# Four accumulating banks in the first feed-forward block of a phase, two in the first projection slab

## The reference

```python
def swiglu(x, wi, wo):
    g, u = jnp.split(x @ wi, 2, axis=-1)
    return (jax.nn.silu(g) * u) @ wo

def ffn_half(h, m, k, g_norm, wi, wo):
    hn = modulate(rmsnorm_2(h, g_norm), m[3 * k], m[3 * k + 1])
    return h + 0.5 * m[3 * k + 2][:, None, :] * swiglu(hn, wi, wo)
...
        h = ffn_half(h, ml, 0, norm_g[l, 0], ffn_wi[l, 0], ffn_wo[l, 0])
        hc = ffn_half(hc, mc, 0, norm_g[l, 0], ffn_wi[l, 0], ffn_wo[l, 0])
        hn = modulate(rmsnorm_2(h, norm_g[l, 1]), ml[3], ml[4])
        hcn = modulate(rmsnorm_2(hc, norm_g[l, 1]), mc[3], mc[4])
        qa, ka, va, qb, kb, vb, uc, gl = project_tokens(hn, w_in[l], qk_g[l], cos, sin)
...
        h = h + ml[5][:, None, :] * merge_branches(ya, yb, yc, gl, w_branch[l], w_out[l])
        h = ffn_half(h, ml, 2, norm_g[l, 2], ffn_wi[l, 1], ffn_wo[l, 1])
```

## Time and profile before

| | us |
|---|---|
| median of 3 runs (lowest, highest) | 3204.87 (3204.76, 3206.72) |
| profiled execution | 3209.25 |
| its span | 3207.5 |
| TensorE matmul busy | 2942.4 (92%) |
| TensorE weight loads busy | 2384.5 (74%) |
| VectorE busy | 1560.7 (49%) |
| ScalarE busy | 1030.6 (32%) |
| GpSimd busy | 273.1 (9%) |

### The profile page before, as it was taken

The page is one execution under the profiler, slowest core; times in us unless marked ns, Lnnn a source line. Parts: engine busy times, 40 slices in busy tenths (PEclk is TensorE's granted clock), DMA queues, the critical chain, the costliest instruction groups (busy, mean ns, idle before and its releaser), DMA issues.

```text
span 3207.5 us, 54730 instructions
## 1 busy us (share of the span) xinstructions
PE 2942.4 (92%) x23653; PEld 2384.5 (74%) x23653; DVE 1560.7 (49%) x2194; ACT 1030.6 (32%) x1502; POOL 273.1 (9%) x201
## 2 busy tenths in 40 slices
PE   6998877899999989899899989999899997989899
PEld 6776565677767679777568868888688886669899
DVE  6524244232223366663764434444544457486566
ACT  3211113222222254532642332222422224264443
POOL 5123000000000000122100000000000012210000
PEclk9988888899999989999999999999999998999899
DMA  6346767999889845411012222222222221104452
GB/s 242 132 149 261 319 249 312 417 372 372 348 349 383 357 174 184 145 66 40 1 40 105 105 92 100 98 92 92 79 92 92 98 99 66 53 14 191 178 189 87
DMA packets 77067, 547.78 MB, mean 171 GB/s; under 512 B 8385, under 2 KB 10433, under 8 KB 11057
## 3 DMA queue, kind: packets, MB, share of 16 engines
q1 hardware_dynamic: 76000, 540.05, 43.4%
q0 software_dynamic: 848, 4.52, 0.4%
HBM read 637.86 MB, written 1.05 MB: 199 GB/s over the span
## 4 chain that ended last, share of the span: by engine, by line
PE 80%; DVE 11%; ACT 4%; DMA 4%; issue 1%; POOL 1%; DVEq 0%; SPq 0%; POOLq 0%; ACTq 0%
PE bank L743 58%; PE bank L1087 8%; DMA ring<-slabs 3%; PE bank L1409 2%; DVE clow L2471 1%; ACT whi L1853 1%; ACT ht L1657 1%; PE bank L792 1%; DVE tiny L2624 1%; PE bank L922 1%; PE bank L909 1%; PE bank L1497 1%; PE bank L759 1%; DVE wk L2601 1%; PE bank L1478 1%
## 5 line engine op out<-in xcount | busy, mean ns | idle before, releaser
L743 PE MATMUL bank<-hhi,whi 128*128 128x256 f32 (+1 forms) x1408 | 482.1, 342 | 31.0 <-DVE hlo L2105 30.9
L743 PE MATMUL bank<-hlo,whi 128*128 128x256 f32 (+1 forms) x1408 | 476.8, 339 | 0.0
L743 PE MATMUL bank<-hhi,wlo 128*128 128x256 f32 (+1 forms) x1408 | 472.9, 336 | 0.0
L2085 DVE TENSOR_TENSOR wlo<-ring,whi 128x2048 fp32r<-128x2048 f32 x132 | 298.7, 2288 | 223.9 <-ACT whi L1612 197.0
L743 PE MATMUL bank<-fhl,whi 128*128 128x256 f32 (+1 forms) x1408 | 351.6, 341 | 0.0
L743 PEld LDWEIGHTS bank<-hhi,whi 128*128 128x128 f32 x1408 | 267.0, 190 | 70.7 <-issue 29.6
L1612 ACT ACTIVATE whi<-ring 128x2048 fp32r<-128x2048 f32 x132 | 251.3, 1908 | 211.5 <-PE bank L743 211.3
L743 PEld LDWEIGHTS bank<-hhi,wlo 128*128 128x128 f32 x1408 | 268.3, 191 | 30.1
L743 PEld LDWEIGHTS bank<-hlo,whi 128*128 128x128 f32 x1408 | 268.4, 191 | 26.2
L1087 PE MATMUL bank<-ring,wk 128*32 128x256 f32 x4064 | 253.5, 392 | 22.9 <-DMA ring<-slabs 14.3
L743 PEld LDWEIGHTS bank<-fhl,whi 128*128 128x128 f32 x1408 | 241.0, 189 | 35.3 <-issue 5.3
(11 more groups left out here) (479 smaller groups left out, 5349.9 us busy)
## 6 DMA issues: line engine op xcount, KB each, us to landing
ring<-slabs SPq DMA_DIRECT2D x542, 1024.0 KB
wk<-slabs SPq DMA_DIRECT2D x45, 1024.0 KB, 11.5
ac<-slabs SPq DMA_DIRECT2D x16, 1024.0 KB, 11.3
wk<-mixp POOLq DMA_DIRECT2D x1, 1040.0 KB, 12.5
xt<-xT SPq DMA_DIRECT2D x1, 1024.0 KB, 6.7
xt<-ctxT POOLq DMA_DIRECT2D x1, 1024.0 KB, 6.1
out<-xt SPq DMA_DIRECT2D x4, 256.0 KB, 2.4
cst<-maskc POOLq DMA_DIRECT2D x1, 960.0 KB, 14.6
```

The costliest lines, as they stand in the source:

```text
L743: last = pe.matmul(o, a, b, start=k == 0, stop=k == len(pairs) - 1)
L2085: tt_(wlo_of(n), slab(n), whi_of(rel).bitcast(F32), ALU.subtract).then_inc(sem("wlo"), 1)
```

## The change

**Feed-forward, TensorE.** Block 0 of every phase becomes `first_block`: it waits for the low parts of both slabs, then goes over the channel tiles outermost, and for each does 8 matmuls with `hhi` (four banks, high and low weight) once `hh` is there, and 4 with `hlo` once `hl` is there. All four banks close with the last four matmuls. The counts of both slabs are paid with the first matmul of block 1.

**Projection, TensorE.** Tiles 0 and 1 are made together in the same way (`project_first`): 4 matmuls with `xhi` and 2 with `hlo` for each channel tile. The sum of squares of tile 0, which stood behind tile 1's matmuls, now stands behind the `lam` matmul.

**Low parts, VectorE.** The low part of slab 1, made after the norm before, is now made ahead of it with that of slab 0. For norm 3 both stand ahead of the reciprocal; for the phases after the output projections they stand after the drains of j = 4 and 5; for the third phase they stand in the last down slab of the second, ahead of drains 0 and 4.

```diff
                         group(bank[bank0 + ft][:, 0:T], pairs3, signal,
-                              ("hl", ph["h0"]) if b == bank0 == ft == 0 and i is None else None)
+                        group(bank[bank0 + ft][:, 0:T], pairs3, signal)
                     used(1)
+
+                def first_block():
+
+                    pe.wait_ge(sem("wlo"), w0 + 2)
+                    for k in range(KT):
+                        parts = [(bank[2 * rel + ft][:, 0:T], *halves(rel, k, ft * P, KT))
+                                 for rel in range(2) for ft in range(FT)]
+                        pe.wait_ge(sem("hh"), ph["h0"] + k + 1)
+                        for o, hi, lo in parts:
+                            mm = pe.matmul(o, hi, HHI[:, k, 0:T], start=k == 0, stop=False)
...
+                            pe.matmul(o, lo, HHI[:, k, 0:T], start=False, stop=False)
+                        pe.wait_ge(sem("hl"), ph["h0"] + k + 1)
+                        for n, (o, hi, lo) in enumerate(parts):
+                            mm = pe.matmul(o, hi, HLO[:, k, 0:T], start=False, stop=k == KT - 1)
+                            if k == KT - 1:
+                                mm.then_inc(sem("gg" if n < FT else "uu"), 1)
+                    used(2)
...
                 def step(b, i):
+                    if b == 0:
+                        first_block()
+                        return
...
+                def project_first():
+
+                    pe.wait_ge(sem("al"), count("al", N_ATT * l + 1))
+                    parts = [(bank[QB[half]][:, 0:tq], *thirds(0, half, tq)) for half in range(2)]
+                    for k in range(KT):
+                        pe.wait_ge(sem("hh"), x0 + k + 1)
+                        for o, hh, lh, hl in parts:
+                            mm = pe.matmul(o, *hh[k], start=k == 0, stop=False)
...
+                            pe.matmul(o, *lh[k], start=False, stop=False)
+                        pe.wait_ge(sem("hl"), x0 + k + 1)
+                        for o, hh, lh, hl in parts:
+                            mm = pe.matmul(o, *hl[k], start=False, stop=k == KT - 1)
+                            if k == KT - 1:
+                                mm.then_inc(sem("qp"), 1)
+                    pe.wait_ge(sem("lam"), l + 1)
+                    pe.matmul(bank[6][:, 0:2], BO64, LAMV[:, 0:2], start=True, stop=True).then_inc(sem("lamd"), 1)
+                    used(1)
...
-                    project(i)
+                    if i == 0:
+                        project_first()
+                    elif i > 1:
+                        project(i)
...
-                if ph is not None:
+                if n == 3:
                     split_slab(ph, 0)
+                    split_slab(ph, 1)
...
-                    if ph is not None:
-                        split_slab(ph, 1)
...
+                        if after is not None and b == ph["nb"] - 1 and m in (0, 4):
+                            split_slab(after, m // 4)
...
+                    if j in (4, 5):
+                        split_slab(PH[2 * l + 1], j - 4)
...
-                ffn(PH[2 * l + 1])
+                ffn(PH[2 * l + 1], None if l else PH[2])
```

More of the change, by code:

```diff
@@ L1277, in first_layer @@
                             pairs3 += [(hi, HHI[:, k, 0:T]), (hi, HLO[:, k, 0:T]), (lo, HHI[:, k, 0:T])]
[L1278 to L1279 removed]
+                        group(bank[bank0 + ft][:, 0:T], pairs3, signal)
                     used(1)
+                def first_block():
[6 more added lines that the diff above has]
+                            mm = pe.matmul(o, hi, HHI[:, k, 0:T], start=k == 0, stop=False)
+                            if owed[0]:
+                                mm.then_inc(sem("slab_used"), owed[0])
+                                owed[0] = 0
+                            pe.matmul(o, lo, HHI[:, k, 0:T], start=False, stop=False)
[5 more added lines that the diff above has]
+                    used(2)
                 def down(b, i):
@@ L1349, in project @@
                     hh, lh, hl = thirds(s, half, T)
-                    if i == 0:
-                        for k in range(KT):
-                            pe.wait_ge(sem("hh"), x0 + k + 1)
-                            mm = pe.matmul(bank[QB[0]][:, 0:T], *hh[k], start=k == 0, stop=False)
-                            if k == 0:
-                                mm.then_inc(sem("slab_used"), owed[0])
-                                owed[0] = 0
-                            pe.matmul(bank[QB[0]][:, 0:T], *lh[k], start=False, stop=False)
-                        for k in range(KT):
-                            pe.wait_ge(sem("hl"), x0 + k + 1)
-                            mm = pe.matmul(bank[QB[0]][:, 0:T], *hl[k], start=False, stop=k == KT - 1)
-                        mm.then_inc(sem("qp"), 1)
-                        pe.wait_ge(sem("lam"), l + 1)
-                        pe.matmul(bank[6][:, 0:2], BO64, LAMV[:, 0:2], start=True, stop=True).then_inc(sem("lamd"), 1)
-                    else:
-                        group(bank[QB[i % 3]][:, 0:T], hh + lh + hl, "qp")
+                    group(bank[QB[i % 3]][:, 0:T], hh + lh + hl, "qp")
                     if half:
@@ L2509, in _, with ffn @@
             dve.tensor_copy(TW[:, 0, :], TW[:, 1, :]).then_inc(sem("xr"), 1)
-            def ffn(ph):
+            def ffn(ph, after=None):
                 T, q0, m0, a0, nd = ph["T"], ph["q0"], ph["m0"], ph["a0"], ph["nd"]
```

4 lines of the change are left out of this document (3 added, 1 removed).

## The result

| | before | after |
|---|---|---|
| median of the runs, us | 3204.82 (3201.68 to 3211.15, 8 runs) | 3212.26 (3206.69 to 3219.69, 8 runs) |
| profiled execution, us (span) | 3209.25 (3207.5) | 3209.54 (3207.7) |

The ratio is 1.0020, with a 95% interval from 1.0012 to 1.0029: the changed kernel is slower by some 4 to 9 us, about as much as a measurement of this kernel can tell from nothing. Forecast were 3210.2 us and a range from 3199 to 3220.

The account below looks back on a forecast made before the run. TensorE, 80% of the chain, was taken to bound the kernel. Block 0 −13.3, gaps +19.4, clock +7.6, drain +0.8, projections −9.2 make +5.3 us on 3204.9: 3210.2 us, range 3199 to 3220.

Parts of the forecast that it names:

- The gap: Behind block 0 in four phases, TensorE waits for slab 2's low part, 4.8 to 4.9 us each; adds 19.4 us.
- Block 0: After norms 3, 5, 6 and 8, TensorE starts earlier and runs 96 matmuls without a stop; gains 13.3 us.
- The clock behind the gaps: Behind each of four gaps, half clock for 4.2 us, 1.9 us lost each; adds 7.6 us.
- The drain: Low parts in the second phase's last down slab delay the first drain and TensorE's first sum; adds 0.8 us.
- The projections: Tile 2 starts 6.0 us earlier after norm 4, tile 0's rotation 3.2 us earlier after norm 7; gains 9.2 us.
- The sum: Whole kernel: all gains and costs together, +5.3 us, giving 3210.2 us.
- No new gap (A): Behind block 0, slab 2 is ready at its end, so gap and clock costs vanish; 3183.2 us, chance 0.06.
- The clock holds (B): Behind block 0, gaps come but the clock does not fall; 3202.6 us, chance 0.12.
- The clock comes back late (C): Behind gaps and in block 0 at 256 columns, half clock lasts 8.20 us; +10.6, 3220.8 us, chance 0.20.
- The projections give less (D): Tile 0's square stays in the open or the clock stays at half after norm 4; 3215 us, chance 0.12.
- The banks (E): In block 0, matmuls in turn over four banks never bring full clock; 3259 us, chance 0.02.

Follow-up runs that it names:

- Experiment 1: Changed kernel with ScalarE's high part of slab 2 ahead of block 0's two activations; 3183.21 us, ratio 0.9934.
- experiment 7: Kernel before with only ScalarE's high part of slab 2 moved ahead of block 0's activations; 3205.55 us, ratio 0.9994.
- experiment 3: Kernel before with only the projection part, tiles 0 and 1 made together; 3204.38 us, ratio 1.0001.
- experiment 5: Kernel before with only VectorE's low parts of slabs 0 and 1 moved ahead of the norms; 3205.75 us, ratio 1.0006.
- Experiment 8: Kernel of experiment 3 plus one unused matmul per job from the 17th on in layer 0's attention; 3197.22 us, ratio 0.9975.
- 10: Kernel of experiment 3 unchanged, one more single execution with a profile; 3208.05 us.
- 11: Kernel of experiment 3 unchanged, a third single execution with a profile; 3186.12 us.
- experiment 4: Changed kernel with filler matmuls, whose results nobody reads, in the gap behind block 0; 3204.83 us, ratio 1.0011.
- experiment 6: Kernel of experiment 1 with the third phase's low parts ahead of drains 3 and 5 instead of 0 and 4; 3186.92 us, ratio 0.9945.
- 2: Changed kernel with the projections put back as before, so the feed-forward part alone; 3218.21 us, ratio 1.0052.
- experiment 9: Kernel of experiment 1 plus the unused matmuls in layer 0's attention; 3190.46 us, ratio 0.9949.

## Why the prediction came out right, and where it was off

**The gap: right, by its own steps.** From the start of block 0's last matmul to the restart it is 4.90, 5.10, 5.11 and 4.89 us; less the one matmul step that was there before, 19.3 us against 19.4 forecast. The chain is the one that the prediction laid out. Experiment 1 changes only ScalarE's order, and the four gaps go but for 0.3 to 0.4 us each; experiment 7 shows that the same edit is worth nothing where the gaps are not: the cause is shown, not argued.

**Block 0: right.** Counted from the norm's last sum, TensorE is through with block 0 2.6, 3.5, 3.9 and 2.9 us earlier than before: 12.7 in all (rounded) against 13.3. What is missing is in part the start: the first matmul comes 0.5, 0.7, 0.7 and 0.7 us earlier than before, where 0.6 to 0.9 were forecast. The clock missed both ways. Without stops, full clock came 4.9 and 2.9 us after the start at 256 columns (4.5 taken) and 3.9 and 3.2 at 512 (the forecast's 1900.2 is 4.1 us after its start at 1896.1). This differs from one execution to the next: in the seven profiles with the old block 0 (before, 3, 5, 7, 8, 10, 11) its last matmul starts from 20.1 to 20.8 us after norm 3's last sum, and from 20.2 to 22.0 after norm 8's. The means of those seven against the six with the new one give 2.5, 3.2, 3.6 and 3.0 us, 12.4 in all, so the 12.7 of one pair of profiles is no accident.

**The clock behind the gaps: right in kind, too small.** It was taken as 4.2 us at half, 1.9 us lost each, 7.6 in all. The stretches are 3.6 to 5.8 us, 5.1 in the mean, which at the same 45% gives 9.2. Filler matmuls brought back 9.4 (experiment 4). The error is the size of the stretch: it was put nearer block 0's 3.22 us than the 5.40 behind an idle stretch in the earlier trace rows, which was the better witness. (That idle stretch was 3.73 us long by before's timeline, not 4.0: the last matmuls ran into it.)

**The drain: right.** 0.8 us forecast, 0.8 in experiment 5 and 0.7 given back in experiment 6.

**The projections: right near the place, partly lost later.** In after's chain of waits (start, us, what) behind norms 4 and 7, ScalarE squares tile 0, TensorE sums the square (L1406) and goes on to tile 2, and later rotates tile 0 (L1413):

```profile
1362.36 0.50 ACT wk L1986
1362.90 1.12 PE bank L1406 x2
1364.03 5.59 PE bank L743 x24
2682.15 0.70 PE bank L1413 x2
```

Tile 2 starts 6.1 us earlier after norm 4's last sum than in the earlier trace rows (6.0 forecast), the rotation after norm 7 3.8 earlier (3.2). After norm 4 full clock came 3.2 us after the start (4 taken). But norm 5 comes only 4.2 us earlier. In the kernel with the projection part alone the lead over before is 6.3 us at 1510 us and 4.5 at 1570, in before's time; in after it is 6.1 and 4.3. Between them after and experiment 3 have a stretch at half clock that before has not (first after's; then the same place of the work in experiment 5, whose projection is before's):

```profile
1519.60:1523.00 3.40, 3.32 (x14) 2.35 (x15) 1.80 (x7) 2.21 (x8) 0.00 (x0) 0.51 0.01 2
```

```profile
1529.30:1532.70 3.40, 3.40 (x20) 2.67 (x19) 0.84 (x2) 1.74 (x6) 0.00 (x0) 0.50 0.03 7
```

The lead falls by 1.5 us there. Experiment 1's execution has no half clock at this place; it starts with a lead of 5.2 us and keeps it. But experiments 5 and 7 have it with the projection of before: they too fall back by 1.5 to 1.6 us there and get 0.9 of it back where a later stretch at half clock is shorter than before's. So the loss is the clock's, and it isn't shown that the new projection brings it. The prediction took the stage as a chain that moves as a whole; it does in work, not in clock.

**The sum.** With what was measured it is −12.7 + 19.3 + 9.4 + 0.8 − 8.5 = +8.3 us, against 8.5 in the profiled executions and +6.4 (3.8 to 9.3) by the ratio, where +5.3 was forecast. Of the 3.0 us between the sums 1.8 are the clock's, 0.7 the projections' and 0.6 block 0's, less 0.1 of the gap. So the forecast is right by its mechanism, with every term of the right sign, and the terms that it missed by most, the clock and the projections, both missed to the same side.

**The rivals.** No new gap (A) is refuted here, but its price was close once the order is changed: 21.7 us under before by A, 21.1 by the ratio of experiment 1 and 20.6 in its profile. That the times agree to a hundredth (3183.2 by A, 3183.21 measured) is luck: experiment 1's runs of before had a median of 3203.4, not 3204.9, and A's price of the clock was 1.8 us too low. The clock holds (B) is refuted by the windows; its price, 7.6, is 9.4. The clock comes back late (C) was put at 8.2 us a stretch, and 5 was named as its point of decision: three of four stretches are past 5, none near 8. By that point the mean of 5.1 lies on C's side; by C's own 8.2 it is nearer to the forecast's 4.2. The projections give less (D) holds between norms 4 and 5, where 1.8 us less came than forecast. The banks (E) are refuted in block 0's windows, with 1.00 over 75 and 88 matmuls in turn over four banks, and in experiment 1; the earlier trace rows, cited against E, hold only one pair of sums and could not have decided it. The Trainium skill ("TensorE: Matmul & The Clock Gate", "A second HAM failure mode: psum-queue depth-cycling") describes a kernel that goes through banks in each iteration and loses its clock by short idle times of TensorE between the groups. Block 0 has no such idle times, so the windows here do not show this loss, and they show that banks in turn do not bring it by themselves.

**What stays open.** Experiment 3 shows the projection part worth nothing in the median, some 7 us in the lower group's times, and 11 in its profile from norm 3 on. Layer 0's attention falls to half clock for 24 us more in some executions of kernels with this part (seen in the profiles of experiments 4 and 10) and in no profile of a kernel without it (before, 2, 5, 7); those are few profiles. Whether some of after's own 8 runs have it is not known, since only one was profiled. What tips it is not settled. Experiment 8 was the test of more work for TensorE there; its times are lower than experiment 3's by the ratios (intervals apart), but its only profile has the stretch no shorter, and experiment 9 shows no gain. That the two groups of times are this half clock rests on one profile with a time of the upper group (10) and on experiment 4's.

## What to carry to other kernels

Where a loop order is changed so that several accumulations close together instead of one after the other, list what stands in the consumers' queues *behind* the instruction that waits for the first of them. A preparation for the next block that used to lie under matmuls moves into the open, though no row of the old profile shows it waiting. It costs a few lines to put it ahead, and here they were worth 28 to 29 us and turned a loss into a gain of 21. Four new gaps of some 5 us on TensorE cost their length here, 19.3 us, and about half as much again, 9.4, for the clock behind them.

Where executions differ by more than the effect, compare stretches between landmarks, and not spans: two nearly equal spans hid a difference of 8.5 us here.

## What the runs showed of the hardware

- After idle stretches of 4.6 to 4.7 us in work at full clock, the granted clock was at half for 3.6 to 5.8 us with TensorE busy throughout, 1.6 to 2.7 us lost each by experiment 4. Matmuls with unused results in the idle time kept it at 1.00.
- One and the same idle stretch of 2.2 us in layer 0's attention (ended at 1518.56 in after) was followed by half clock for 3.4 us in the profiles of after and of experiments 3, 5 and 7, and by none in those of before and experiment 1. Kernels with and without the change are on either side, so the change doesn't decide it.
- One and the same program runs layer 0's attention in 538.3 or 547.4 us from norm to norm, the longer with 24 us more at half clock. Experiment 3's times lie in two groups 7 us apart, with the median of the 12 runs between them; this stretch may be what parts them, which two profiles support and none proves.
